# A hybrid decoder layer on one core: the next tile's weight split placed behind a tile's first third, and a reordered end

## What is computed

```
h    = concat(meta, x)                                   # (1040, 1024)
proj = rmsnorm(h, norm1) @ w_in                          # 8 blocks of 1024 and more: q, k, v, z, gates, retention q, k, v, g
y_a  = gated delta rule over chunks, from silu(conv4(q, k, v)), normed, * silu(z)
y_b  = retention over chunks, from rotary(q), rotary(k), v, normed, * silu(g)
h    = h + (sigmoid(gate_a) * y_a + sigmoid(gate_b) * y_b) @ w_out
u    = conv3(rmsnorm(h, norm2) @ w_up) + b               # 2 * 2816 columns
h    = h + (silu(a) * b) @ w_down                        # a, b = halves of u
out  = rmsnorm(h, norm_f)[16:]
```

## Time and profile before

| | |
|---|---|
| median of three runs | 2081.26 us |
| the profiled execution | 2082.35 us, its span 2080.6 us |
| TensorE matmul busy | 2038.6 us, 98% of the span |
| VectorE, ScalarE, GpSimd busy | 1179.2, 627.9, 289.6 us |
| mean granted TensorE clock | 0.996 |
| high split, L1206 | 125 times, 1056 ns |
| low split, L1502 | 125 times, 1266 ns |
| eviction, L1280 | 207 times, 457 ns |

### The profile page before, as it was taken

The page is one execution under the profiler, slowest core; times in us unless marked ns, Lnnn a source line. Parts: engine busy times, 40 slices in busy tenths (PEclk is TensorE's granted clock), DMA queues, the critical chain, the costliest instruction groups (busy, mean ns, idle before and its releaser), DMA issues.

```text
span 2080.6 us, 30407 instructions
## 1 busy us (share of the span) xinstructions
PE 2038.6 (98%) x12936; PEld 1952.9 (94%) x12936; DVE 1179.2 (57%) x1357; ACT 627.9 (30%) x794; POOL 289.6 (14%) x277
## 2 busy tenths in 40 slices
PE   8999999999999999999999999999999999999997
PEld 7999998999999999999999999999999999999995
DVE  6457574656677647665434343466565656565556
ACT  5223333434333544344433332211111111111112
POOL 0000002659280222222000002000000000000002
PEclk9999999999999999999999999999999999999999
DMA  9235566554555754645152211111011101111102
GB/s 279 92 103 134 134 164 196 181 193 153 172 153 133 170 178 135 187 146 164 51 185 101 103 62 51 61 61 52 31 51 51 51 31 55 53 56 37 45 31 81
DMA packets 252204, 227.11 MB, mean 109 GB/s; under 512 B 141102, under 2 KB 209622, under 8 KB 251942
## 3 DMA queue, kind: packets, MB, share of 16 engines
q1 hardware_dynamic: 252070, 225.17, 35.7%
HBM read 161.29 MB, written 63.84 MB: 108 GB/s over the span
## 4 chain that ended last, share of the span: by engine, by line
PE 87%; DVE 3%; SPq 3%; DMA 3%; ACT 2%; issue 2%; POOL 0%; POOLq 0%; DVEq 0%; ACTq 0%
PE a_psum L886 32%; PE a_psum L145 29%; PE a_psum L1154 11%; PE a_psum L873 4%; DMA w_raw<-in_w_in 2%; PE a_psum L961 1%; PE a_psum L979 1%; SPq L641 1%; PE a_psum L1062 1%; PE a_psum L943 1%; PE a_psum L1005 1%; PE a_psum L958 1%; PE a_psum L989 1%; PE a_psum L1077 1%; PE a_psum L1046 1%
## 5 line engine op out<-in xcount | busy, mean ns | idle before, releaser
L886 PE MATMUL a_psum<-xh,w_hi 128*128 128x348 f32 (+1 forms) x1656 | 538.2, 325 | 8.1 <-ACT post L1280 8.1
L886 PE MATMUL a_psum<-xl,w_hi 128*128 128x348 f32 (+1 forms) x1656 | 533.1, 322 | 0.0
L886 PE MATMUL a_psum<-xh,w_lo 128*128 128x348 f32 (+1 forms) x1656 | 531.5, 321 | 0.0
L886 PEld LDWEIGHTS a_psum<-xh,w_hi 128*128 128x128 f32 x1656 | 313.0, 189 | 12.6 <-ACT post L1280 9.6
L886 PEld LDWEIGHTS a_psum<-xl,w_hi 128*128 128x128 f32 x1656 | 313.3, 189 | 1.0
L886 PEld LDWEIGHTS a_psum<-xh,w_lo 128*128 128x128 f32 x1656 | 313.1, 189 | 0.0
L1206 ACT ACTIVATE w_hi<-w_raw 128x1024 fp32r<-128x1024 f32 x125 | 132.0, 1056 | 473.8 <-PE a_psum L145 409.4
L145 PE MATMUL a_psum<-xh,w_hi 128*128 128x342 f32 (+1 forms) x1152 | 245.1, 321 | 9.0 <-DVE xl L1524 9.0
L1280 ACT ACTIVATE post<-a_psum 128x348 f32<-128x348 f32 (+1 forms) x207 | 94.2, 457 | 512.7 <-PE a_psum L886 492.9
L145 PE MATMUL a_psum<-xl,w_hi 128*128 128x342 f32 (+1 forms) x1152 | 244.8, 321 | 0.0
L145 PE MATMUL a_psum<-xh,w_lo 128*128 128x342 f32 (+1 forms) x1152 | 244.0, 320 | 0.0
(11 more groups left out here) (239 smaller groups left out, 2807.2 us busy)
## 6 DMA issues: line engine op xcount, KB each, us to landing
w_raw<-in_w_in SPq DMA_DIRECT2D x76, 512.0 KB, 3.9
w_raw<-in_w_up SPq DMA_DIRECT2D x44, 512.0 KB, 3.5
mix_scratch<-post SPq DMA_DIRECT2D x32, 522.0 KB, 2.8
down_raw<-in_w_ffn_down SPq DMA_DIRECT2D x22, 512.0 KB, 4.4
ext<-mix_scratch SPq DMA_DIRECT2D x9, 1024.0 KB, 7.5
y<-mix_scratch SPq DMA_DIRECT2D x18, 512.0 KB, 5.5
ext<-grow_scratch SPq DMA_DIRECT2D x9, 512.0 KB, 4.9
ext<-mix_scratch SPq DMA_DIRECT2D x9, 512.0 KB, 6.3
```

What stands on the lines that cost most here:

```text
L886: mm = pe.matmul(psum[:, u % 2, 0:n], w[:, k, :], x[:, k, at0 + n * j:at0 + n * j + n], start=(k == 0 and part == 0), stop=(k == KC - 1 an ...
```

## The change

Three edits. In the plan, the unit stands ahead of the splits that share its place, so ScalarE evicts the unit first and makes the high split after it. At the last up pair, VectorE makes the adds 154, 155 and 156 ahead of the split of the activations, and TensorE's waits in the last two groups of down products follow the bank that each product writes. In the final norm GpSimd sums blocks 0 to 5, the squares of blocks 6 and 7 get buffers of their own, and TensorE adds both with a matmul each.

```diff
     def unit(t, j):
+        add(("proj", t, j))
         if j == 0 and not T_RV - 1 <= t < T_Q - 1:
             add(("split", t + 1))
         for n in splits_at.get((t, j), ()):
             add(("split", n))
-        add(("proj", t, j))
...
-        o_sqb, o_sum2, o_sq7 = ([x[:, 512 * n:512 * n + 512] for n in range(2)] for x in post[0:3])
+        o_sqb, o_sum2, *o_sq67 = ([x[:, 512 * n:512 * n + 512] for n in range(2)] for x in post[0:4])
...
-                    pe.wait_ge(added, base + (0, 0, 0, 0, 0, 1, 4, 5)[n - base])
+
+                    pe.wait_ge(added, base + ((-2, -6, -5, -1, 0, 1, 4, 5) if last else (0, 0, 0, 0, 0, 1, 4, 5))[n - base])
...
             def sums(half):
-                pe.wait_ge(o_sum, 6 * half + 6)
+                pe.wait_ge(o_sum, 5 * half + 5)
                 pe.matmul(psum[:, 3 + half, :], ones, o_sum2[half], start=True, stop=False)
-                pe.wait_ge(o_sqd, 8 * half + 8)
-                pe.matmul(psum[:, 3 + half, :], ones, o_sq7[half], start=False, stop=True).then_inc(o_ss, 1)
+                for n in range(2):
+                    pe.wait_ge(o_sqd, 8 * half + 7 + n)
+                    mm = pe.matmul(psum[:, 3 + half, :], ones, o_sq67[half][n], start=False, stop=(n == 1))
+                mm.then_inc(o_ss, 1)
...
-                into = o_sum2[half] if m == 0 else o_sq7[half] if m == KC - 1 else o_sqb[m % 2]
+                into = o_sum2[half] if m == 0 else o_sq67[half][m - 6] if m >= 6 else o_sqb[m % 2]
...
                 if last:
                     gate_product(j)
-                    adds(2)
+                    adds(2, 3, 4)
                     split_act(j)
                     split_down(j, *(x[(t + 1) % 2].rearrange("p k c -> p (k c)") for x in (wh, wl)))
-                    adds(3, 4, 5, 6, 7)
+                    adds(5, 6, 7)
...
-                for m in range(1, KC - 1):
+                for m in range(1, KC - 2):
                     pool.wait_ge(o_sqd, 8 * half + m + 1)
                     if m > 1:
-                        pool.wait_ge(o_sum, 6 * half + m - 1)
+                        pool.wait_ge(o_sum, 5 * half + m - 1)
```

More of the change, by code:

```diff
@@ L1471, in square @@
                 act.wait_ge(added, 8 * FT + 8 * (half - 2) + m + 1)
-                into = o_sum2[half] if m == 0 else o_sq7[half] if m == KC - 1 else o_sqb[m % 2]
+                into = o_sum2[half] if m == 0 else o_sq67[half][m - 6] if m >= 6 else o_sqb[m % 2]
                 if m == 0 and half == 0:
                     act.wait_ge(act_lo, FT)
-                if 0 < m < KC - 1:
+                if 0 < m < KC - 2:
                     if m >= 3 or half:
-                        act.wait_ge(o_sum, 6 * half + max(m - 2, 0))
+                        act.wait_ge(o_sum, 5 * half + max(m - 2, 0))
                 act.activation(into, half_of(m, half), ACT.Square).then_inc(o_sqd, 1)
```

## The result

| | before | changed |
|---|---|---|
| median of six runs each | 2081.66 us | 2070.76 us |
| lowest to highest | 2079.49 to 2083.84 | 2069.70 to 2071.92 |
| the profiled execution | 2082.35, span 2080.6 | 2070.83, span 2069.0 |
| mean granted clock | 0.996 | 0.998 |

The ratio is 0.9940, 95% interval 0.9931 to 0.9950: 12.5 us saved by the ratio, 10.9 by the medians. The forecast was 2070.9, a gain of 10.4, with a range of 2067 to 2077.

What follows compares the result with a forecast made beforehand. TensorE, with 87% of the path that ended last, was taken to bound the kernel. Front 8.6 − 2.0 − 0.2 = 6.4 plus end 4.0 gave 10.4 us: profiled 2071.95, median 2070.9, range 2067 to 2077.

Steps and rivals of the forecast that it cites:

- Tile 2: Front, tile 2: its eviction stall goes with the split behind the first unit; gain 0.5 us.
- Tile 18: Front: unit (18, 2) starts 2.64 us earlier and at full clock, with 0.3 to spare at tile 19; gain 4.0.
- Tile 67: A wait of 1.0 us at tile 68 replaces 3.48 of stall and 1.7 of slow clock; gain 4.1.
- Tiles 48 and 49: Their stalls, 1.5 us together, give nothing: tile 49's low split stands behind VectorE's convolution and its chain holds the first chunk.
- L1005 in 52 and 62: Delta rule's tiles: the later low split delays this TensorE line, costing 0.8 us in each tile.
- L1046 in 55: Delta rule's tile 55: low split and `on` behind it come later, so this waiting line does too; cost 0.4 us.
- Around tile 25: Four splits move in a row; stores behind later transposes delay TensorE 0 to 1.4 us; taken as 0.2.
- The clock gives nothing back: Rival: the two slow stretches, 1.4 and 1.7 us, reappear behind the new waits; 2074.0 us; chance 0.12.
- The chunks pay more: Rival: late low splits cost 0.84 us in all ten delayed delta tiles, 8.4 instead of 2.0; 2077.3 us; chance 0.12.
- Slower: Rival: VectorE is held by the low split, 0.84 us lost in 27 tiles, 22.7 in all; 2091.6 us; chance 0.04.
- The end does not give: Rival: add 157 and two splits stay last, ones-matmul eats the rest; end gives 1, not 4; 2073.9 us; chance 0.09.
- The rule on the clock: Clock changes vary between runs, so the profile's 3.1 us of half clock need not lie in timed runs; new waits may meet one.

Runs made afterwards that it cites:

- stalled_only: Kernel before, with the split of the next weights behind the first unit only in tiles 2, 18, 48, 49 and 67; 2075.19 us, ratio 0.9952.
- delta_ahead: Changed kernel, with the split ahead of the first unit again in tiles 50 to 66 and from 68 on; 2069.80 us, ratio 0.9933 to before.
- one_unit_later: Kernel before, with the split behind the second unit in tiles from 17 on (24 to 32: behind their units), end unchanged; 2098.49 us, ratio 1.0065.
- front_only: Kernel before with only the split of the next weights moved behind the first unit, end unchanged; 2076.03 us, ratio 0.9968.
- squares: Kernel before with only the final norm's change, TensorE summing the last two squares by a third ones-matmul; 2084.31 us, ratio 1.0005.
- waits_alone: Kernel before with only TensorE's waits by bank in the last down block, order of the adds unchanged; 2081.23 us, ratio 0.9985.
- best_of_parts: Kernel before with late splits in tiles 2 to 49 and 67, adds ahead, waits by bank, and the squares' edit in the second half only; 2068.12 us, ratio 0.9920.

## Why the prediction was right, and where it was off

**Edit 1, 6.4 forecast.** The first trace gives 7.6. But one trace of each is a poor ruler, as the rows of all fourteen traces show. TensorE's 7200th instruction starts at 1077.4 to 1079.4 in the six kernels with the old front (mean 1078.4), at 1070.2 to 1070.4 in the three with edit 1: 8.1 us, with a spread of 2 in the old fronts, as their evictions' stalls vary (tile 67: 3.25 to 4.15; tile 48: 0.84 to 3.28). The terms, as the lead of the changed kernel has them:

- *Tile 2, 0.5:* 0.6.
- *Tile 18, 4.0:* the lead rose from 0.7 to 4.7, so 4.0. The mechanism as forecast, no wait in tile 19.
- *Tile 67, 4.1 with a new wait of 1.0:* the lead rose by 5.1 and fell by 0.35 with a wait of 0.29, so 4.7; in the other traces with edit 1 everywhere the wait was 0.95 and 1.23, which is the 1.0.
- *Tiles 48 and 49, 0:* this term was mis-sized. Both evictions' stalls went (0.93 and 0.60), and tile 49 began 1.03 late behind the low split. The step saw that the split can't come sooner, but took for granted that the chain behind it holds the first chunk; TensorE came out 1.0 ahead and kept it.
- *L1005 in 52 and 62, 0.8 each; L1046 in 55, 0.4:* 0.49, 0.49 and 0.34 more of wait, in lead 0.55, 0.66 and 0.32. `stalled_only` and `delta_ahead` show by their absence that the late split is the cause. The lag of 2.07 taken from tile 57 held (757.11 to 759.19, 2.08); the low split came 0.2 sooner than counted, half of it because ScalarE begins the high split 0.11 before the eviction's record ends. Tile 57 stayed at 0.84, as forecast.
- *Around tile 25, 0.2:* nothing was lost there.

**What the sum did not hold.** The wait in tile 30 (+1.5) stood in three of the six old fronts (1.10, 1.22, 0.68) and in none of the seven fronts with late splits (all but `one_unit_later`), that in tile 33 (−0.9) in one of these seven. Whether edit 1 removes the first stays open: three of six against none of seven is short of proof, and `stalled_only`, which leaves the splits around tile 25 where they were, hasn't it either. The longer wait of L1005 for `y` (−0.7) is no steady cost: that wait is 0.34 to 1.18 in the six old fronts and 0.64 to 1.85 in the seven with late splits. The wait in tile 37 (−1.3) comes with either front: eleven of thirteen traces have it, 1.0 to 1.2 each, five of the six old fronts among them. The profile of before was one of the two that have not. What decides it is told below.

**Edit 2, 4.3; edit 3, −0.9 and +0.5; together 4.0.** Measured 4.39, −0.86 and +0.57, together 4.10. The wait before product 160 was 0.49 for 0.7, the last wait for GpSimd's sum 0.10. The room of VectorE behind it, counted at 0.83 and unchanged, came out at 0.28: TensorE's part shrank by 0.55 more than VectorE's. It still covered; half a microsecond more of gain there would have found it gone.

**The rivals.** *The clock gives nothing back* falls: ahead of the last 20 us, the six old fronts have three or four stretches at 1.2 GHz each, the changed kernel's two traces one each. No kernel with late splits has one behind tile 18 or 67, and none has one behind the new waits in tiles 49 and 68. *The chunks pay more* falls: 1.5 was paid, not 8.4. *Slower* falls, and `one_unit_later` shows how far off it was: one more unit of delay, in tiles that had 4.8 us to spare. *The end does not give* falls: 4.1.

The rule on the clock did bear on this kernel, though in another way than weighed. Of the six traces with a stall of 2.76 us before product 158, three have a stretch at 1.2 GHz behind it (`front_only`, `squares`, `stalled_only`) and three have none (before, `waits_alone`, `one_unit_later`). The stall of tile 18 (2.2 to 2.75) has one behind it in four of the six old fronts and none in `squares` and `waits_alone`, that of tile 67 in all six. So of the 3.1 us of half clock that the rule put in doubt, tile 67's share was met each time and tile 18's was not, and one profile without such a stretch doesn't say that a stall is free of it. The Trainium skill, page "TensorE: Matmul & The Clock Gate", section "What's actually happening", says that where the clock changes varies between runs of one kernel. These traces agree. Edit 2 was worth 4.4 against before's profiled execution and 5.6 to 5.9 against the three whose clock fell there. An estimate from these rows is 8.1 for the front, 4.1 for the end, and 0.7 for a fall of 1.2 to 1.5 in half of the executions, 12.9 together. The ratios (0.9940, 0.9938) give 12.5 and 12.9, while the sum from one trace was 10.4 and the medians of the first six runs gave 10.9. That the varying stalls and the clock make up this difference fits, but is not shown. That the forecast of 2070.9 met the median of 2070.76 so closely is luck: in the front, unforecast steps of −1.4 together stood against terms that came out 2.6 better than counted (tiles 48 and 49 by 1.0, tile 67 by 0.6, tiles 52 and 62 by 0.4, the rest small), and the clock's share of the end was in no sum.

## What to carry to other kernels

Move a step only where it removes a stall: five tiles brought all of the gain, and the same edit cost 1.5 us of waits where the moved work stood ahead of something on the chain. When in-order engines share a step list, ask of each place what stands right behind the moved step on the next engine. And a sum at the scale of 1 us needs more than one trace: rows that differ between executions of kernels with the same code there are neither gain nor cost.

## What the runs showed of the hardware

**Who starts first decides 1.2 us.** In tile 37 VectorE multiplies two halves of `y` (L1641), while GpSimd, released by a DMA at almost the same time, multiplies 1024 columns (L1983). In before, VectorE started 0.07 ahead and took 0.69; GpSimd took 2.48. VectorE's row, then GpSimd's:

```profile
486.73 0.69 DVE L1641 TENSOR_TENSOR y<-y 128x512 f32<-128x512 f32 x1 [8.57 <-ACT y L1340]
...
486.80 2.48 POOL L1983 TENSOR_TENSOR y<-ext,a_cst 128x1024 f32<-128x1024 f32 x1 [0.30 <-DMA ext<-mix_scratch]
```

In the changed kernel GpSimd started 0.05 ahead and took 2.00; VectorE took 2.49, and TensorE stood 1.23 at its L979 behind it:

```profile
481.48 2.49 DVE L1644 TENSOR_TENSOR y<-y 128x512 f32<-128x512 f32 x1 [8.58 <-ACT y L1343]
...
481.43 2.00 POOL L1986 TENSOR_TENSOR y<-ext,a_cst 128x1024 f32<-128x1024 f32 x1 [0.22 <-DMA ext<-mix_scratch]
...
487.17 1.10 PE L979 MATMUL a_psum<-ext,y 128*128 128x256 f32 x4 [1.23 <-DVE ext L1666]
```

It is so in all thirteen traces (all but `one_unit_later`, whose steps meet elsewhere): in the two where VectorE was first (before by 0.07, `best_of_parts` by 0.10) it took 0.69 and TensorE did not wait; in the eleven where GpSimd was first, by 0.04 to 0.29, VectorE ended 0.55 after GpSimd and TensorE waited 1.0 to 1.2. The same two lines meet at three more places in each of these traces; VectorE starts about 0.95 behind there, takes about 1.60, and again ends 0.55 after GpSimd. The Trainium skill, page "SBUF — State Buffer", section "Who interferes with whom", says that a VectorE instruction with two inputs in SBUF and a GpSimd instruction that reads SBUF exclude each other, and that the one issued second waits for the whole of the first; these rows agree. The luck of that order, not the change, made the largest unforecast loss in the trace.

**The clock fell with no long stall ahead of it.** Near 691 us in all seven traces with late splits, near 696 in four of the old fronts (the other two fell at 705 behind a longer stall of tile 48), and near 830 in seven traces, TensorE went to 1.2 GHz where it had worked through small matmuls with gaps between them, none over 1.42 us. The changed kernel, a stretch ahead of the fall and one behind it; the clock column is the last but two:

```profile
686.20:691.20 5.00, 3.79 (x29) 3.50 (x28) 2.14 (x3) 4.69 (x5) 0.71 (x1) 1.00 1.04 207
691.20:694.20 3.00, 3.00 (x12) 3.00 (x12) 0.79 (x2) 0.00 (x0) 3.00 (x2) 0.50 0.78 158
```
